# A gated memory's stabiliser rows spread over 128 partitions by one rounded product instead of a float32 one, the first head's scores one block later

## The reference, cut to what matters

```python
bcum = jnp.cumsum(lf, axis=-1)
dmat = bcum[..., :, None] - bcum[..., None, :] + li[..., None, :]
dmat = jnp.where(tril, dmat, -jnp.inf)
m_inter = bcum + m_st[..., None]
m_t = jnp.maximum(m_inter, jnp.max(dmat, axis=-1))
s_qk = jnp.einsum('bhtd,bhsd->bhts', qx, kx) * jnp.exp(dmat - m_t[..., None])
```

## Time and profile before

| | us |
|---|---|
| median of 3 runs | 2207.69 |
| lowest, highest | 2207.23, 2213.12 |
| span of the profiled execution | 2206.6 |
| PE busy | 2185.9 (99%) |
| DVE busy | 1492.7 (68%) |
| ACT busy | 1013.1 (46%) |
| POOL busy | 266.0 (12%) |

### The profile page before, as it was taken

The page is one execution under the profiler, slowest core; times in us unless marked ns, Lnnn a source line. Parts: engine busy times, 40 slices in busy tenths (PEclk is TensorE's granted clock), DMA queues, the critical chain, the costliest instruction groups (busy, mean ns, idle before and its releaser), DMA issues.

```text
span 2206.6 us, 32483 instructions
## 1 busy us (share of the span) xinstructions
PE 2185.9 (99%) x10910; PEld 1849.9 (84%) x10910; DVE 1492.7 (68%) x1995; ACT 1013.1 (46%) x1246; POOL 266.0 (12%) x499
## 2 busy tenths in 40 slices
PE   9999999999999999999999999999999999999998
PEld 8898889988878887898888888888888888888886
DVE  5766668877777878587776768775566655444544
ACT  5445545444444445444555444454444444443433
POOL 2101110112210010701111211110000100000000
PEclk9999999999999999999999999999999999999999
DMA  8867576778986594968666877756776776565564
GB/s 294 246 194 233 177 271 232 194 247 292 304 282 182 164 313 141 262 201 263 220 193 198 294 262 244 250 199 225 237 233 218 255 239 210 176 224 181 186 200 138
DMA packets 200428, 500.72 MB, mean 227 GB/s; under 512 B 31816, under 2 KB 59112, under 8 KB 200048
## 3 DMA queue, kind: packets, MB, share of 16 engines
q1 hardware_dynamic: 166256, 394.10, 55.4%
q0 software_dynamic: 33760, 104.41, 14.9%
q10 hardware_dynamic: 288, 0.52, 0.1%
HBM read 496.84 MB, written 2.15 MB: 226 GB/s over the span
## 4 chain that ended last, share of the span: by engine, by line
PE 90%; DMA 4%; DVE 3%; ACT 1%; issue 1%; POOLq 0%; DVEq 0%; SPq 0%; ACTq 0%
PE ps L2251 73%; PE ps L2295 10%; DMA ada_raw<-in_w_ada_dram 2%; DMA raw<-in_ml_w_in_dram 1%; DVE lo L1225 1%; PE ps L2348 1%; PE ps L2719 1%; PE ps L2708 1%; DVE acc_s L1237 0%; PE ps L2609 0%; PE ps L2791 0%; DVE acc_g L1237 0%; PE ps L2443 0%; PE ps L2444 0%; PE ps L2466 0%
## 5 line engine op out<-in xcount | busy, mean ns | idle before, releaser
L1225 DVE TENSOR_TENSOR lo<-raw,hi 128x1024 fp32r<-128x1024 f32 x731 | 889.7, 1223 | 550.1 <-ACT hi L667 547.6
L667 ACT CAST hi<-raw 128x1024 fp32r<-128x1024 f32 x731 | 763.7, 1052 | 964.4 <-PE ps L2251 742.7
L2251 PE MATMUL ps<-hi,XH 128*128 128x512 f32 x1944 | 609.3, 393 | 3.6 <-DVE lo L1225 1.4
L2251 PE MATMUL ps<-lo,XH 128*128 128x512 f32 x1944 | 602.6, 390 | 0.0
L2251 PE MATMUL ps<-hi,XL 128*128 128x512 f32 x1944 | 602.0, 390 | 0.0
L2251 PEld LDWEIGHTS ps<-hi,XL 128*128 128x128 f32 x1944 | 365.0, 188 | 76.7
L2251 PEld LDWEIGHTS ps<-lo,XH 128*128 128x128 f32 x1944 | 365.0, 188 | 76.5
L2251 PEld LDWEIGHTS ps<-hi,XH 128*128 128x128 f32 x1944 | 360.8, 188 | 78.2 <-issue 4.1
L585 POOL DMA_DIRECT2D ada_raw<-in_w_ada_dram x384 | 206.5, 539 | 1552.2 <-DVE acc_s L1237 895.2
L1237 DVE SCALAR_TENSOR_TENSOR acc_s<-ada_raw,c_act,acc_s 128x512 f32<-128x512 f32 x256 | 191.1, 747 | 20.9 <-DMA ada_raw<-in_w_ada_dram 19.6
L2295 PE MATMUL ps<-XH,hi 128*128 (+1 forms) x504 | 142.9, 284 | 0.0
(11 more groups left out here) (385 smaller groups left out, 1833.1 us busy)
## 6 DMA issues: line engine op xcount, KB each, us to landing
ada_raw<-in_w_ada_dram POOLq DMA_DIRECT2D x384, 256.0 KB, 4.7
raw<-in_w_in_dram SPq DMA_DIRECT2D x136, 512.0 KB, 4.4
raw<-in_ml_w_in_dram SPq DMA_DIRECT2D x128, 512.0 KB, 4.7
raw<-in_w_gate_dram SPq DMA_DIRECT2D x176, 256.0 KB, 2.9
raw<-in_w_up_dram SPq DMA_DIRECT2D x176, 256.0 KB, 3.7
raw<-in_w_down_dram SPq DMA_DIRECT2D x88, 512.0 KB, 4.0
raw<-in_mla_w_in_dram SPq DMA_DIRECT2D x47, 512.0 KB, 4.9
raw<-in_mla_w_out_dram SPq DMA_DIRECT2D x32, 512.0 KB, 4.5
```

Source lines behind the costliest of these rows:

```text
L667: nc.scalar.copy(hi[:, j, :], raw[:, j, :]).then_inc(hi_ready, 1)
L1225: nc.vector.tensor_tensor(lo[:, j, :], raw[:, j, :], hi[:, j, :].bitcast(F32), ALU.subtract) \
L2251: ins = mm(ps[:, o:o + HALF], x, w[:, b % RING, c0:c0 + HALF], start=first, stop=(k == n_rows - 1 and x is xl), skip_group_check=True)
```

## The change

- `select` becomes a rounded tile of 128 rows with ones in rows h and 32 + h. DVE makes it as the sum of two spread slices of `ident`, behind the fourth lo of mo_0's stage; its constant, its DMA and the wait for it go.
- A tile `ge_parts` (128 rows, rounded) takes the place of `ge` in the product: DVE sets it to zero behind the stabiliser's last step (`ge_zero`), ACT copies -M rounded into rows 0 to 7 in front of mo_0's casts (`ge_hi`), and DVE writes the remainder into rows 32 to 39 behind the fourth lo of mo_0's stage. Two events `heads_ready` stand for both tiles.
- `prepare_heads` and `head_scores(0)` move from behind block 0 to behind block 1 of mz0.
- The events for the first half and the first three quarters of a stage, one semaphore each so far, share two semaphores with counts (`half_of`, `three_of`).

The diff, cut to its core:

```diff
-                  ("cos", 128), ("sin", 128), ("select", 1024)):
+                  ("cos", 128), ("sin", 128)):
...
-        select = at("select", 195.5, [8, ML_H, P])
+        select = at("select", 195.5, [P, ML_H, P], F32R)
...
+        ge_parts = at("ge_parts", 128, [P, SEQ], F32R)
...
+        HALVES = ("z0", "mo1", "lo1", "ga0", "ga1", "ob1", "wo1", "down1")
+        THREES = ("mo1", "down1")
+
+        def half_of(name):
+
+            return ev("first_half"), HALVES.index(name) + 1
...
-            load("select", select[:, :, :].rearrange(flat), cst("select", 0, 8))
...
             act.wait_ge(ev("stabiliser"), 1)
             nc.scalar.activation(gF[:, :], gF[:, :], ACT.Exp, scale=-1.0).then_inc(ev("exp_m"), 1)
+            act.wait_ge(ev("ge_zero"), 1)
+            nc.scalar.copy(ge_parts[0:8, :], ge[:, :]).then_inc(ev("ge_hi"), 1)
             first4(B_VOZ + 32)
...
             nc.vector.tensor_tensor(gF[:, :], gF[:, :], gM[:, :], ALU.add).then_inc(ev("stabiliser"), 1)
+            nc.vector.memset(ge_parts[:, :].bitcast(F32), 0.0).then_inc(ev("ge_zero"), 1)
             rest(B_VOZ + 16, 16, "mv1")
             first4(B_VOZ + 32)
+            dve.wait_ge(ev("ge_hi"), 1)
+            nc.vector.tensor_tensor(ge_parts[32:40, :], ge[:, :], ge_parts[0:8, :].bitcast(F32), ALU.subtract) \
+              .then_inc(ev("heads_ready"), 1)
+            one, two = (ident[:, o:o + ML_H].unsqueeze(2).broadcast_to([P, ML_H, P]) for o in (0, 32))
+            nc.vector.tensor_tensor(select[:, :, :], one, two, ALU.add).then_inc(ev("heads_ready"), 1)
             rest(B_VOZ + 32, 16, "mo_0")
...
-                    ins.then_inc(ev(name + "_half"), 1)
+                    ins.then_inc(ev("first_half"), 1)
...
-                pe.wait_ge(ev("select"), 16)
+                pe.wait_ge(ev("heads_ready"), 2)
                 pe.wait_ge(ev("qk"), 16)
...
-                mm(ps[:, b:b + SEQ], select[:, h, :], ge[:, :], start=True, stop=True,
+                mm(ps[:, b:b + SEQ], select[:, h, :], ge_parts[:, :], start=True, stop=True,
                    skip_group_check=True).then_inc(M2["bc"], 1)
...
             def heads_after(b):
-                if b == 0:
+                if b == 1:
                     prepare_heads()
                     head_scores(0)
...
-    put("select", np.repeat(np.eye(8), P, axis=1), 8)
```

More of the change, by code:

```diff
@@ L352, in col, with three_of @@
             return pk[:, o:o + 1]
+        HALVES = ("z0", "mo1", "lo1", "ga0", "ga1", "ob1", "wo1", "down1")
+        THREES = ("mo1", "down1")
+        def half_of(name):
+            return ev("first_half"), HALVES.index(name) + 1
+        def three_of(name):
+            return ev("three_quarters"), THREES.index(name) + 1
         def complete(name):
@@ L861, in _ @@
                 if k == 7:
-                    act.wait_ge(ev("z0_half"), 1)
+                    act.wait_ge(*half_of("z0"))
                     nc.scalar.copy(z_tok[:, 0, 0:COLS], T("z0", 0)).then_inc(ev("z0_freed0"), 1)
@@ L1086, in gate_half @@
                 if tok == 0:
-                    act.wait_ge(ev(name + "_half"), 1)
+                    act.wait_ge(*half_of(name))
                     nc.scalar.copy(dst[:, 0, :], T(name, 0)).then_inc(ev(name + "_freed0"), 1)
@@ L1373, in last_residual @@
                 if tok == 0:
-                    dve.wait_ge(ev(name + "_half"), 1)
+                    dve.wait_ge(*half_of(name))
                 else:
@@ L1651, in quarter @@
                     mark(nc.vector.bn_stats(st[:, tok, 2 + cc, :], xs))
-            quarter("mo1", 0, (0, 1), (ev("mo1_half"), 1))
-            quarter("mo1", 1, (0,), (ev("mo1_three"), 1))
+            quarter("mo1", 0, (0, 1), half_of("mo1"))
+            quarter("mo1", 1, (0,), three_of("mo1"))
             def statistics(tok):
@@ L2100, in _ @@
                             split_merged("mTa", 0)
-                        dve.wait_ge(*(complete(name) if tok else (ev("ob1_half"), 1)))
+                        dve.wait_ge(*(complete(name) if tok else half_of("ob1")))
                     v = sig[q][:, tok, :]
@@ L2143, in _ @@
             rest(B_WO + 16, 16, "wo1")
-            dve.wait_ge(ev("wo1_half"), 1)
+            dve.wait_ge(*half_of("wo1"))
             gated_token("wo1", 1, 0, g_row, "x3")
@@ L2196, in _ @@
             rest(B_DOWN + KF, KF, g0=2)
-            dve.wait_ge(ev("down1_half"), 1)
+            dve.wait_ge(*half_of("down1"))
             gated_token("down1", 1, 0, g2_row, "x4")
@@ L2204, in last_quarter @@
             def last_quarter(c):
-                dve.wait_ge(*(complete("down1") if c else (ev("down1_three"), 1)))
+                dve.wait_ge(*(complete("down1") if c else three_of("down1")))
                 cols_ = slice(COLS + c * HALF, COLS + (c + 1) * HALF)
@@ L2285, in token_major @@
                             ins = token_part(g, nb, H, L, b, 1, cs=(0,))
-                        ins.then_inc(ev(name + "_three"), 1)
+                        ins.then_inc(ev("three_quarters"), 1)
                     for b in range(b1 - RING, b1):
@@ L2500, in z_part @@
                 elif b == 15:
-                    ins.then_inc(ev("z0_half"), 1)
+                    ins.then_inc(ev("first_half"), 1)
             def out_part(b, tok):
```

## The result

| | before | after |
|---|---|---|
| median of 11 runs each, us | 2208.07 | 2213.65 |
| lowest, highest, us | 2206.63, 2213.12 | 2212.53, 2215.54 |
| span of the profiled execution, us | 2206.6 | 2212.6 |

The account below looks back on a forecast made before the run. The prediction took TensorE, busy 99% of the span, as the bound. Its terms 4.9 + 1.8 - 0.35 = 6.35 us took 2207.69 to 2201.3 us, with a range of 2199.7 to 2204.6.

Parts of the forecast that it names:

- TensorE in heads 1 to 7: Stabiliser's product and scores of each head: 0.70 us less a head, 4.9 us for seven; lower end 2.2.
- The first head: Between mz0's first blocks: block 1 fills PE's wait for ScalarE, gain 1.8 us, bounds 1.3 and 1.8.
- (a): Heads: the pauses aren't due to the rows and stay; gain 3.5 us, 2204.2 us; chance 0.12.
- (c): Heads: drains go, but the two products' weight loads stay in the open; gain 4.75 us, 2202.9 us; chance 0.05.
- VectorE and ScalarE: Added steps in the stages of mv1 and mo_0: cost 0.35 us, bounds 0 and 2.3.
- The gain lasts: Behind the heads: all work is released by PE in turn and moves with it.
- rival (d): 145 us before the heads: smaller constants move weights, transfers 10% longer, PE waits up to 14.5 us; 2215.8 us; chance 0.05.

Follow-up runs that it names:

- the two kernels that part rows from format: After with 1024 unused constant columns: the product on 128 rows in plain float32, 2204.52 us; or rounded over 8 rows, 2205.98 us.
- the step alone: Before, with prepare_heads and head_scores(0) behind block 1 instead of block 0, nothing else: 2206.73 us, ratio 0.9986.
- before with small constants: Before, with select as an input of its own behind all others and the constants without it: 2220.05 us, ratio 1.0049.
- 2048 columns more: After with 2048 unused columns in the constant matrix, 1462 KB in all: 2203.61 us, ratio 0.9977.

## Why the prediction was wrong

**TensorE in heads 1 to 7: right.** 0.70 us a head was predicted from two pauses of 0.2 and a pass structure read off the starts; 2.77 - 2.07 = 0.70 was measured, and the two kernels that part rows from format give the pauses to the rows. Rivals (a) (groups at 13.4) and (c) (13.2) fall: they are at 13.00.

**The first head: right, 2.1 for 1.8.** With the step alone the stretch is 1.6 us shorter; that kernel still has the old product in the first head. In after the heads give 7.0, of which seven times 0.70 is 4.9, and 2.1 are left. The section came to 0.34 + 0.31 + 0.43 + 0.22 = 1.30 in the chain, where the sum had 1.57. The drain that the sum put ahead of the transposes is in the piece before: its 24 products take 5.72 us where the next 24 take 5.49, and the load behind them has 0.35 of idle before it. `head_values(0)` doesn't wait, as reckoned. Heads together: 6.7 predicted, and 6.9 to 7.0 measured by PE's products in every kernel that has both steps whole. One reserve: the 1.5 us of waiting for ACT that before's profile has is not fixed (0.4 in another profile of the same order).

**VectorE and ScalarE: 0.35 predicted, too little to be seen.** The memset, the subtraction and the addition took 0.27, 0.42 and 1.23 us, and the copy 0.39, as their rows said. Twice the work moved PE's waits by 0.7 us and its starts by 0.9, inside the spread of kernels that have it once. The 0.35 is neither confirmed nor refuted.

**The gain lasts, nearly.** All kernels with the new code give back 0.3 to 0.9 us behind the heads, after by +0.5; the three with before's product don't (0.0, 0.0 and -0.1). By the chains it goes in one place, between 850 and 856 us of before, where the later block's input is normalised and PE waits for VectorE and ScalarE in turn. In the chain of after VectorE spends 0.40 us in `issue` ahead of `ss` (L1903), where in before it is 0.04; the rest follows at the transposes behind it. Why it does stays open. The prediction had it that all work behind the heads moves with PE.

**The step that failed is the term that the sum left at nothing: what the smaller constant matrix does to the transfers.** It measured +10.4 us by PE's products (6.0 at the gate columns, 4.4 in v and o). The prediction had it as rival (d) alone, and there its chance and its place were wrong. The mechanism was named: the constants shrink, the weights lie elsewhere, transfers take longer, PE waits for lo. It got 0.05, because "Nothing in the trace speaks for it beyond the thin stock". But that sentence is true of every effect of placement: the trace of before holds one placement and can't speak on another. And the price was put where the stock of lo is thin, in the 145 us before the heads, while the larger part came where a load already took long: `small_raw` lands in 10.4 us in before, the longest block load beside it in 12.5 where the median is 4.3. Those rows were there to be read, in a stretch that the change doesn't touch, and so wasn't looked at. In the 145 us themselves the landing of `raw` went from a median of 5.6 us to 5.9, about 5% where (d) supposed 10%, and the loss was 4.1 us where (d) had 14.5. The median is a weak guide to it: it is 5.4 to 5.7 us in the kernels that lose nothing there and 5.8 to 5.9 in those that lose 3 to 4.5, but 5.6 in before with small constants, which loses 2.5. That transfers in this stretch land later is thus shown less well than for the gate columns. That (d)'s 2215.8 lies close to 2213.65 is luck: it had 14.5 for 4.1, and nothing for the 6.4 at the gate columns.

The sum of the terms as measured in after is -7.0 for the heads, +6.4 for the gate columns, +4.1 for v and o, +0.5 behind, and +1.5 + 0.4 before the 137th block: +5.9, of the 6.0 by which the profiled spans differ. Without the constants' part, the forecast of -6.35 us stands beside -0.36%, -0.22%, -0.23% and -0.24% in the four kernels with constants above 512 KB and nothing else changed, -5.8 us in the mean: inside the forecast's own range.

The +1.5 at the start is PE's clock, which comes up later in this execution. The products in order of time (start, us, engine, line), of before:

```profile
7.09 0.62 PE L2391 MATMUL ps<-lo,XH 128*128 128x512 f32 x2
7.55 0.62 PE L2391 MATMUL ps<-hi,XH 128*128 128x512 f32 x2
```

and of after:

```profile
7.36 1.05 PE L2410 MATMUL ps<-hi,XL 128*128 128x512 f32 x2
8.21 1.05 PE L2410 MATMUL ps<-lo,XH 128*128 128x512 f32 x2
```

Pairs start 0.85 us apart instead of 0.46. The trace records the full clock from 9.6 us on, against 5.1 in before (ahead of that it has no record, and windows print 1.00). In six of the eighteen profiles it comes at 9.6 to 10.7 us, and they lose 1.5 to 2.0 us there; in the others it comes at 4.0 to 6.7. Small and large constants are in both groups, and so is the new code; the four profiles of before's code all have it early. What sets the moment stays open. Two of the others lose 1.0 and 1.5 by a wait of PE for `lo` near 12 us (the added work made twice, and 2048 columns more), the rest lose -0.1 to +0.4. With one profile a kernel this limits what a ledger's sum can tell to some 2 us; the stretches behind it are not touched.

## What to carry to other kernels

An edit that removes or shrinks an input can change how long the transfers of other inputs take, and no profile of the kernel before can exclude it. Time it with the input padded to its old size as well: one such run parts the code's effect from that of the input's size, and here it turned a loss of 0.2% into a gain of 0.22 to 0.36%. For a small product between large ones, keep the row count of its neighbours: going from 128 rows to 8 and back cost 0.4 us a head, more than the product's own work (0.12), and the idle time ahead of the weight loads shows it.

## What was not expected of the hardware

- The size of one input moved the landing times of other tensors in a step between 512,000 and 544,768 bytes: 16.0 us against 9.8 for the same load, 2212.82 us against 2204.71 for the kernel.
- Two loads of 2048 pieces of 32 bytes held up the block loads of another queue: 19.4 us for 512 KB where the median is 4.7, at 117 GB/s with the DMA engines 0.67 busy. The Trainium skill, DMA: Bandwidth & Descriptors (why small descriptors are slow), gives each packet a fixed cost, so that small pieces load the engines more than their bytes say. The trace agrees that pieces matter (one 512 KB load in rows of 4 KB lands in 5.1 us). Why the same pieces take 10 us in one kernel and 16 in another no run here shows.
- One stall of 4.3 us cost PE 6.0: the granted clock behind it was 0.50 for 3.4 us, which is 1.7 us more.
- At the start of the program the full clock came at 4.0 to 6.7 us in twelve profiles and at 9.6 to 10.7 in six, which costs such an execution 1.5 to 2.0 us.
